# Routing written out with one-hot lists, and expert combination fused into the q/k/v projection, in a two-block transformer kernel on one Trainium2 core

## The chip, the cores and the metric

The kernel is one program on 1 core of one Trainium2 chip. The metric is the device time of one execution in microseconds (us), the median of several executions.

## The reference

1024 tokens of width 1024, all in float32. A first block mixes the tokens (latent attention and an RWKV branch), adds the product with `w_out`, normalises, and sends each token through 2 of 32 experts; a second block has windowed attention, a recurrent layer and 16 experts that choose their tokens. The part that the change touches is this:

```python
x = x + mixed @ w_out                       # x1
h2 = rms_norm(x, norm_ffn_g)
# hier_moe: best of 4 groups, best 2 of its 8 experts
group_p = softmax(h2 @ rg_w + rg_b); e_logits = h2 @ re_w + re_b
weight = gp[:, None] * tp / sum(tp); expert = gi * 8 + ti
# tokens sorted by expert, each expert's list padded to blocks of 128
slot_tok = full(cap, T).at[dest].set(stok)
y_block = (silu(xb @ w1[e]) * (xb @ w3[e])) @ w2[e]
x = x + segment_sum(yb * slot_w, slot_tok)
x = rms_norm(x, norm_final_g)               # x2, end of the first block
qkv = x @ attn_w_qkv                        # second block: rotary, window of 128, sink
x = layer_norm(ALPHA * x + attention @ attn_w_o) ...
```

## The kernel before, in words

`P = 128` tokens are a tile, `NT = 8` tiles, `KD = 8` slices of 128 of the width, `HALF = 512` columns. The program is a row of stages. Each is a `Phase`: it allocates tiles and semaphores, runs one block in which every engine (TensorE, VectorE = DVE, ScalarE = ACT, GpSimd = POOL, SyncE = SP) has its own instruction list, and ends by clearing its semaphores and a barrier of all engines (line 83 shows in the trace for it). `hold` waits on a semaphore; `link` waits for the instruction just issued, so linked vector operations run one by one. `sp.dma_start` puts a transfer on SP's queue, `act.dma_start` on ACT's, `pool.indirect_dma_start` on the software queue.

`route_phase` (L1478). SP issues eight small loads (L1544), then the first two tiles of the mixed activations (L1552), the two halves of `w_out` (L1554), the rest of the activations (L1555), and in a hardware loop x in and x1, h2 out (L1556). POOL copies each tile of activations to `m_t` (L1577). TensorE makes 16 products (128x128 by 128x512) into the one tile `po` (L1604), then turns the h2 of the tile before (8 transposes, L1612) and makes 8 logits products (L1619). The vector engine adds x (L1658), takes the norm with two short ACT steps (L1660 to L1665), scales the turned h2 (L1670) and keeps the logits (L1675). `po`, `x1`, `h2` and `h2T` exist once. When all logits are there, the vector engine makes the choice for the eight tiles at once (L1697 to L1721), three products give each token's rank in its expert (L1632 to L1634), and from it come slot numbers (`slot_u`, L1742), the expert of each block (`block_e`, L1748) and the pairs of blocks in use (`pair_used`, L1751). POOL writes the token numbers to these slots in DRAM with 16 indirect stores (L1589).

`experts_phase` (L1758). For each of up to 48 blocks, two per step: SP loads a column of 128 token numbers (L1810) and, four blocks ahead, the expert's three matrices, 3 MB (L1816, L1818); POOL gathers the 128 rows of h2 (L1823), two blocks ahead; TensorE turns them (L1845), makes 8 gate/up products (L1861), turns the hidden values and makes 4 down products (L1885). Here 32 blocks are in use.

`combine_phase` (L1982). For each tile POOL gathers two rows of results per token (L2024); the vector engine adds them with their weights to x1 (L2047, L2048), ACT takes squares and root, the vector engine normalises (L2066), SP stores x2.

`gqa_project` (L2110). In a loop over tiles: x2 in (L2143), transposes (L2171), a copy (L2235), 24 products in three groups of 512 columns (L2190), between the first and second group the transposes of the heads of the tile before (L2178, L2182); ACT copies q (L2221), the vector engine k and v (L2247, L2248) and rotates q and k (L2257 to L2263). `gqa_attend` (L2271) loads one mask per tile (L2298), its vector work begins at L2392. After it a phase of its own loads the output weights (L3004, called from L2106), and the tail's first products (L2547) wait for them.

## Time and profile before

| | us |
|---|---|
| median of 3 runs | 4951.96 (4951.84 to 4953.2) |
| profiled execution, its own time | 4939.51 |
| its span | 4937.7 |
| TensorE matmul busy | 4243.3 (86%) |
| VectorE busy | 1567.0 (32%) |
| ScalarE busy | 1090.8 (22%) |
| GpSimd busy | 290.2 (6%) |

The profile is of one execution; its time is compared with the runs' median separately. TensorE is busy for 86% of the span, so a stage in which it is idle or at the lower granted clock stands out. Rows of stages give, for each engine, busy time and instruction records (x), then TensorE's granted clock as a share of full speed, the share of the 16 DMA engines, and GB/s. Rows of the timeline give start, duration, engine, line, operation, tiles, and in brackets the idle time before and what ended it.

### The profile page before, as it was taken

To read this page: it belongs to the slowest core of one execution; us is meant where nothing else is said; L and a number is where in the kernel's file an instruction comes from. 1 tells how busy PE (TensorE), PEld (TensorE's weight loads), DVE (VectorE), ACT (ScalarE), POOL (GpSimd) and SP (SyncE) were. 2 spreads that over 40 slices of the span, in tenths; PEclk is the share of its full clock that TensorE was granted. 3 is DMA by queue.
4 is the path that set the end of the run, shared out by engine and by line. 5 is a ranking of instruction groups with operands and counts; after the bars stand their busy time and mean duration, and the time that the engine had idled before them with its cause. 6 is when DMAs were issued, how large, how long until landed. Compare 5 with 4: busy or idle time off the path is not lost. (4 is left out here: it accounts for less than half of the span.)

```text
span 4937.7 us, 63014 instructions
## 1 busy us (share of the span) xinstructions
PE 4243.3 (86%) x23058; PEld 2190.4 (44%) x23059; DVE 1567.0 (32%) x2896; ACT 1090.8 (22%) x1837; POOL 290.2 (6%) x297
## 2 busy tenths in 40 slices
PE   7899996888987849984988969999969995999996
PEld 4555445774433424442444534444434443444442
DVE  3355463542221122223165530110136536100112
ACT  1155223442100101111044300000026522000002
POOL 0000002320000010001000000000000000000000
PEclk9899998999998869997999979999989997999998
DMA  2130145432213139975001458888731133888884
GB/s 90 54 143 24 49 162 135 89 68 77 93 35 115 64 128 370 357 265 208 17 14 72 173 185 311 304 309 313 247 112 43 64 112 131 304 313 309 311 305 174
DMA packets 427020, 820.70 MB, mean 166 GB/s; under 512 B 146640, under 2 KB 288080, under 8 KB 393808
## 3 DMA queue, kind: packets, MB, share of 16 engines
q1 hardware_dynamic: 397968, 717.33, 41.9%
q0 software_dynamic: 17216, 60.83, 4.3%
q10 hardware_dynamic: 11648, 39.88, 2.0%
q8 instruction: 137, 2.24, 0.2%
q14 instruction: 51, 0.42, 0.0%
HBM read 692.09 MB, written 125.86 MB: 166 GB/s over the span
## 5 line engine op out<-in xcount | busy, mean ns | idle before, releaser
L2829 PE MATMUL ec1e_pg<-ec_wg,ec1e_xT 128*128 128x512 f32 x1024 | 445.2, 595 | 2.2 <-DVE ec1e_xT L2882 2.2
L2829 PE MATMUL ec0e_pg<-ec_wg,ec0e_xT 128*128 128x512 f32 x1024 | 444.5, 595 | 2.1 <-DVE ec0e_xT L2882 2.1
L2829 PEld LDWEIGHTS ec1e_pg<-ec_wg,ec1e_xT 128*128 128x128 f32 x1024 | 195.6, 191 | 249.0 <-issue 249.0
L2829 PEld LDWEIGHTS ec0e_pg<-ec_wg,ec0e_xT 128*128 128x128 f32 x1024 | 195.4, 191 | 248.3 <-issue 248.3
L1371 PE MATMUL mix_pb<-h_h_all,mix_wg 128*128 128x512 f32 x512 | 223.3, 597 | 12.2 <-DMA mix_wg<-in_w_in_dram 12.2
L1861 PE MATMUL exp_pg<-exp_wb,exp_xT 128*128 128x512 f32 x512 | 224.9, 598 | 6.4 <-DMA exp_wb<-in_w_dram 6.4
L3113 PE MATMUL lrui_pA<-lrui_xT,lrui_w 128*128 128x512 f32 x512 | 223.1, 595 | 2.6 <-ACT lrui_xT L3187 2.6
L2855 PE MATMUL ec1e_py<-lru_wd,ec1e_hidT 128*128 128x512 f32 x512 | 223.4, 594 | 0.0
L2855 PE MATMUL ec0e_py<-gqaw_wd,ec0e_hidT 128*128 128x512 f32 x512 | 223.4, 594 | 0.0
L679 PE MATMUL front_pz<-h_h_all,front_w 128*128 128x512 f32 x480 | 211.6, 599 | 8.8 <-DMA front_ones<-in_head_ones_dram 8.8
L2190 PE MATMUL gqap_pq<-gqap_w,gqap_xT 128*128 128x512 f32 x384 | 180.7, 631 | 22.4 <-DVE gqap_xT L2235 17.5
L1604 PE MATMUL route_po<-route_wo,route_m_t 128*128 128x512 f32 x256 | 130.8, 676 | 40.9 <-DMA route_wo<-in_w_out_dram 25.3
L2870 ACT ACTIVATE ec1e_sg<-ec1e_pg 128x512 f32<-128x512 f32 x32 | 19.1, 598 | 650.9 <-PE ec1e_pg L2829 650.9
L2870 ACT ACTIVATE ec0e_sg<-ec0e_pg 128x512 f32<-128x512 f32 x32 | 19.1, 598 | 649.8 <-PE ec0e_pg L2829 649.8
L1371 PEld LDWEIGHTS mix_pb<-h_h_all,mix_wg 128*128 128x128 f32 x512 | 98.0, 192 | 135.6 <-issue 135.6
L2890 DVE TENSOR_TENSOR ec0e_hid<-ec0e_sg,ec0e_pg 128x512 f32<-128x512 f32 x32 | 22.0, 689 | 428.1 <-ACT ec0e_sg L2870 428.1
L2890 DVE TENSOR_TENSOR ec1e_hid<-ec1e_sg,ec1e_pg 128x512 f32<-128x512 f32 x32 | 22.0, 688 | 427.3 <-ACT ec1e_sg L2870 427.3
L1861 PEld LDWEIGHTS exp_pg<-exp_wb,exp_xT 128*128 128x128 f32 x512 | 98.1, 192 | 130.2 <-issue 130.2
L3113 PEld LDWEIGHTS lrui_pA<-lrui_xT,lrui_w 128*128 128x128 f32 x512 | 97.6, 191 | 125.1 <-issue 125.1
L972 POOL TENSOR_TENSOR wkv_a_l<-wkv_a_raw,wkv_tab 128x512 f32<-128x512 f32 x80 | 106.4, 1363 | 783.5 <-ACT wkv_a_raw L988 783.5
L679 PEld LDWEIGHTS front_pz<-h_h_all,front_w 128*128 128x128 f32 x480 | 91.3, 192 | 127.1 <-issue 127.1
L2855 PEld LDWEIGHTS ec1e_py<-lru_wd,ec1e_hidT 128*128 128x128 f32 x512 | 96.0, 190 | 115.5 <-issue 114.8
(533 smaller groups left out, 6135.5 us busy)
## 6 DMA issues: line engine op xcount, KB each, us to landing
ec_wg<-in_moe_w_gate_up_dram SPq DMA_DIRECT2D x256, 1024.0 KB, 6.4
exp_wb<-in_w_dram SPq DMA_DIRECT2D x64, 1024.0 KB, 15.2
gqaw_wd<-in_moe_w_down_dram SPq DMA_DIRECT2D x128, 512.0 KB, 4.4
lru_wd<-in_moe_w_down_dram SPq DMA_DIRECT2D x128, 512.0 KB, 4.4
exp_w2b<-in_w_dram SPq DMA_DIRECT2D x32, 1024.0 KB, 14.2
wkv_inp<-arrays SPq DMA_DIRECT2D x160, 128.0 KB, 3.0
arrays<-front_out SPq DMA_DIRECT2D x36, 512.0 KB, 5.7
yb<-mlaa_zero SPq DMA_DIRECT2D x1, 16384.0 KB, 52.8
```

The lines of the kernel that those rows point to most:

```text
L679: m = nc.tensor.matmul(pz[q % 2][:, half * HALF:(half + 1) * HALF], w[:, q % U, k, :], hT[:, k, half * HALF:(half + 1) * HALF], start=k == ...
L972: nc.gpsimd.tensor_tensor(grid(a_l[:, n, :]), grid(a_raw[:, :]), mask(n + 1), ALU.mult).then_inc(a_masked, 1)
L1371: m = nc.tensor.matmul(ps[:, half * HALF:(half + 1) * HALF], weights[:, k, :], rhs[:, k, half * HALF:(half + 1) * HALF], start=k == 0, sto ...
L1604: m = nc.tensor.matmul(po[:, half * HALF:(half + 1) * HALF], m_t[:, k, :], wo[:, k, half * HALF:(half + 1) * HALF], start=k == 0, stop=k = ...
L1861: m = nc.tensor.matmul(pg[:, u, :], xT[:, b, k, :], wb[:, b, :, k, :], start=k == 0, stop=k == KD - 1)
L2190: m = nc.tensor.matmul(pq[:, b, :], xT[:, k, :], w[:, k, b * HALF:(b + 1) * HALF], start=k == 0, stop=k == KD - 1)
L2829: return nc.tensor.matmul(pg[:, b, :], xT[:, k, :], wg[:, k, b * HALF:(b + 1) * HALF], start=k == 0, stop=k == KD - 1)
L2855: m = nc.tensor.matmul(py[:, b * HALF:(b + 1) * HALF], hidT[:, k, :], wd[:, k, b * HALF:(b + 1) * HALF], start=k == 0, stop=k == KD - 1)
L2870: nc.scalar.activation(sg[:, half * HALF:(half + 1) * HALF], pg[:, half, :], ACT.Silu).then_inc(silu, 1)
L2890: nc.vector.tensor_tensor(hid[:, cols], sg[:, cols], pg[:, 2 + half, :], ALU.mult).then_inc(hid_ready, 1)
L3113: m = nc.tensor.matmul(pA[:, bank, :], w[:, q % W_RING, k, :], xT[:, k, halves[h]], start=k == 0, stop=k == KD - 1)
```

## The change: what it does

- Loads of the router: activations first, then each weight half followed by an x tile, then seven small loads. All but the last-named are no longer waited for by the first product.
- The router's loop is written out, without POOL's copy; `po`, `x1`, `h2`, `h2T` double; transposes and logits of a tile stand between the halves of the next one's product; additions go by halves.
- The choice is made for tiles 0 to 5 inside the loop, and for 6 and 7 behind it.
- The experts of the first two blocks are worked out first, and SP loads their weights then. Token lists come from 16 products of one-hot matrices, end in SBUF (`moe.idx`), and POOL gathers the first two blocks' rows in the same phase. In the experts POOL copies an index column before each gather.
- The combination phase goes; its steps stand in the projection, written out by tiles. x2 is turned from SBUF, and stored to DRAM beside that. The gathered rows lie in `oT`, the q weights in the tile `wd`.
- Three kinds of mask in place of eight; output weights are loaded at the start of attention.

```diff
 route_phase, sync:
+                sp.dma_start(mT[:, :, 0:EARLY], mix_view[:, :, 0:EARLY]).then_inc(early, 16)
+                for h in range(2):
+                    sp.dma_start(wo[:, :, halves[h]], w_out[0, :, halves[h]].rearrange("(k p) n -> p k n", p=P)).then_inc(wo_in[h], 16)
+                    sp.dma_start(xt[:, h, :], x[h * P:(h + 1) * P, :]).then_inc(x_in[h], 16)
...
+                sp.wait_ge(first_e, 1)
+                for s in range(2):
+                    e = moe.expert_of(sp, s)
+                    moe.load_gu(sp, s, e)
+                    moe.load_dn(sp, s, e)
 route_phase, gpsimd:
-                    nc.gpsimd.tensor_copy(m_t[:, :, :], mT[:, :, ds(i * P, P)]).then_inc(m_in, 1)
...
-                for n in range(2 * NT):
-                    pool.indirect_dma_start(slot_tok, bass.IndirectOffsetOnAxis(ap=slot_u[:, n:n + 1], axis=0),
-                                            tok[:, n % NT:n % NT + 1], None).then_inc(scattered, 16)
+                pool.wait_ge(idx_ready, 1)
+                for s in range(2):
+                    pool.indirect_dma_start(moe.xg[:, s, :], None, h2_dram, bass.IndirectOffsetOnAxis(ap=moe.idx[:, s:s + 1], axis=0)).then_inc(moe.x_in[s], 16)
 route_phase, tensor:
+                for t in range(NT):
+                    product(t, 0, range(KD))
+                    if t:
+                        turn_h2(t - 1)
+                    product(t, 1, range(KD // 2))
+                    if t:
+                        logits(t - 1)
+                    product(t, 1, range(KD // 2, KD))
...
+                for j in range(2 * NT):
+                    if j % NT == 0:
+                        pe.wait_ge(pos_ready, j // NT + 1)
+                    m = nc.tensor.matmul(pt[:, 0:MOE_BLOCKS], at_pos[:, j, :], in_block[:, j, :], start=j == 0, stop=j == 2 * NT - 1)
 route_phase, vector:
+                for t in range(NT):
+                    norm(t)
+                    if t + 1 < NT:
+                        add(t + 1, 0)
+                    scaled(t)
+                    keep_logits(t)
+                    if t == NT - 3:
+                        choose(0, NT - 2)
+                    if t + 1 < NT:
+                        add(t + 1, 1)
+                choose(NT - 2, NT)
...
+                experts_of(0, 2)
+                dve.sem_inc(first_e, 1)
...
+                V.link(nc.vector.tensor_tensor(in_block[:, :, :], slot_f[:, :].unsqueeze(2).to_broadcast(wide), blocks.unsqueeze(1).to_broadcast(wide), ALU.is_ge))
+                V.link(nc.vector.tensor_reduce(base[:, :], in_block[:, :, :], AX_X, ALU.add))
+                V.link(nc.vector.tensor_scalar(base[:, :], base[:, :], float(P), float(P), ALU.mult, ALU.subtract))
+                V.link(nc.vector.tensor_tensor(pos[:, :], slot_f[:, :], base[:, :], ALU.subtract))
+                V.link(nc.vector.tensor_tensor(in_block[:, :, :], base[:, :].unsqueeze(2).to_broadcast(wide), blocks.unsqueeze(1).to_broadcast(wide), ALU.is_equal))
+                for m in range(2):
+                    mine = slice(m * NT, (m + 1) * NT)
+                    nc.vector.tensor_tensor(in_block[:, mine, :], in_block[:, mine, :],
+                                            tab[:, TAB + P:TAB + P + NT].unsqueeze(2).to_broadcast([P, NT, MOE_BLOCKS]), ALU.mult)
+                dve.sem_inc(in_ready, 1)
+                for m in range(2):
+                    V.link(nc.vector.tensor_tensor(at_pos[:, mine, :], pos[:, mine].unsqueeze(2).to_broadcast([P, NT, P]),
+                                                   tab[:, TAB:TAB + P].unsqueeze(1).to_broadcast([P, NT, P]), ALU.is_equal))
+                    dve.sem_inc(pos_ready, 1)
+                experts_of(2, MOE_BLOCKS)
...
+                dve.wait_ge(i_psum, 1)
+                V.link(nc.vector.tensor_copy(moe.idx[:, 0:MOE_BLOCKS], pt[:, 0:MOE_BLOCKS]))
 experts_phase, sync:
+                def load(i, q, ahead):
+                    for u in range(2):
+                        b = 2 * q + u
+                        e = moe.expert_of(sp, i * R + (b + ahead))
+                        S.hold(gu_psum, done(i, b + ahead - R))
+                        moe.load_gu(sp, b, e)
+                        S.hold(y_psum, done(i, b + ahead - R))
+                        moe.load_dn(sp, b, e)
                 with sp.Fori(0, NB // R) as i:
+                    with sp.If(in_use(sp, i * 2 + 1) > 0):
+                        load(i, 1, 0)
+                    with sp.If(in_use(sp, i * 2 + 2) > 0):
+                        load(i, 0, R)
 experts_phase, gpsimd:
+                                nc.gpsimd.tensor_copy(ic[s][:, :], moe.idx[:, ds(i * R + (b + 2), 1)]).then_inc(ic_ready, 1)
 gqa_project, tensor:
+            for i in range(NT):
+                product(i, 0)
+                if i:
+                    turn_heads(i - 1)
+                product(i, 1)
+                if i + 1 < NT:
+                    turn_x(i + 1)
+                product(i, 2)
 gqa_project, vector:
+            for i in range(NT):
+                if i + 1 < NT:
+                    combined(i + 1)
+                if i:
+                    keep_k(i - 1)
+                if i + 1 < NT:
+                    keep_x(i + 1)
+                copy_kv(i)
+                rotate(i)
 gqa_attend:
-    mask = ph.sb("mask", [P, NT, BAND])
+    mask = ph.sb("mask", [P, 3, BAND])
...
+            load_w_out(sp, wd, w_out, wo_in)
```

`combined(i)` has the operations of L2047, L2048, L2053, L2063 and L2066, in place on x1, and waits for ACT's square and root in it. ACT runs, per tile, the square and root of tile i+1, the copy of the first half of q, the copy of the turned heads of tile i-1, and the second half of q. SP stores x2 of tile i, waits for its transposes, and loads x1 of tile i+4.

## Rows read from the trace of the kernel before

**Rows 1.** Busy time by stage: two router tiles, experts, combination, two projection tiles.
```profile
core 0: us, PE busy (x) PEld busy (x) DVE busy (x) ACT busy (x) POOL busy (x), PEclk, DMA share, GB/s
1589.50:1609.20 19.70, 16.79 (x56) 8.79 (x56) 2.49 (x5) 3.92 (x5) 1.04 (x1) 1.00 0.24 81
1609.20:1633.10 23.90, 19.73 (x56) 9.88 (x56) 3.72 (x6) 3.92 (x5) 1.04 (x1) 0.86 0.18 66
1853.00:1877.00 24.00, 23.79 (x71) 11.56 (x70) 5.81 (x9) 3.23 (x5) 1.90 (x2) 1.00 1.07 375
2220.30:2272.30 52.00, 0.00 (x0) 0.00 (x0) 31.73 (x40) 13.38 (x26) 19.18 (x17) 0.50 0.86 333
2307.00:2332.40 25.40, 23.32 (x73) 11.53 (x72) 5.12 (x19) 2.04 (x3) 0.00 (x0) 1.00 0.06 21
2332.40:2359.70 27.30, 24.67 (x71) 11.77 (x69) 5.12 (x19) 2.01 (x2) 0.00 (x0) 0.94 0.06 19
```

**Rows 2.** Who waited for whom in the router: us in total, times, longest.
```profile
PE route_po L1604 <- DVE route_x L1658: 15.6, 7, 2.4
```

**Rows 3.** Timeline, start of the router, SP's queue and TensorE.
```profile
1555.98 0.35 SPq L1549 DMA_DIRECT2D route_ident<-in_eye_dram  x1
...
1560.44 0.43 SPq L1552 DMA_DIRECT2D route_mT<-mixT  x1
...
1572.58 15.45 PE L1604 MATMUL route_po<-route_wo,route_m_t 128*128 128x512 f32 x32 [25.35 <-DMA route_wo<-in_w_out_dram]
```

**Rows 4.** Timeline, last tile of the router.
```profile
1752.64 1.23 DVE L1658 TENSOR_TENSOR route_x<-route_po,route_xt 128x1024 f32<-128x1024 f32 x1 [0.52 <-issue]
...
1759.00 0.75 DVE L1665 TENSOR_SCALAR route_h<-route_x,route_small 128x1024 f32<-128x1024 f32 x1 [0.37 <-DVE route_small L1662]
...
1763.10 3.62 PE L1619 MATMUL route_pl<-route_rw,route_h2T 128*128 128x36 f32 x16 [1.32 <-DVE route_h2T L1670]
1766.76 0.20 DVE L1675 TENSOR_TENSOR route_lg<-route_pl,route_rb 128x36 f32<-128x36 f32 x1 [3.72 <-PE route_pl L1619]
```

**Rows 5.** Timeline, rank products and slots.
```profile
1777.73 1.22 PE L1632 MATMUL route_pr<-route_mem,route_tab 128*128 128x256 f32 x2 [11.01 <-DVEq L1721]
...
1780.19 0.42 DVE L1731 TENSOR_TENSOR route_over<-route_pl,route_tab 128x256 f32<-128x256 f32 x1 [1.38 <-PE route_pl L1634]
...
1784.41 1.76 DVE L1745 TENSOR_TENSOR route_cmp<-route_pend,route_tab 128x1536 f32<-128x1536 f32 x1 [0.15 <-DVE slots L1742]
```

**Rows 6.** Timeline, token lists to the first expert product.
```profile
1784.61 2.60 POOL L1589 DMA_INDIRECT slot_tok<-route_tok,slots  x1 [60.22 <-DVEq L1743]
...
1813.14 0.98 POOL L1823 DMA_INDIRECT exp_xg<-h,exp_idx  x1 [6.79 <-DMA exp_idx<-slot_tok]
...
1818.23 1.94 PE L1845 MATMUL exp_pt<-exp_ident,exp_xg 128*128 128x128 f32 x8 [38.15 <-DMA exp_xg<-h,exp_idx]
...
1829.95 5.30 PE L1861 MATMUL exp_pg<-exp_wb,exp_xT 128*128 128x512 f32 x6 [6.36 <-DMA exp_wb<-in_w_dram]
```

**Rows 7.** Combination and projection: timeline, and one row of DMA issues (us to landing last).
```profile
2220.32 0.35 SPq L2003 DMA_DIRECT2D comb_g<-in_norm_final_g_dram  x1
...
2232.10 1.28 DVE L2047 SCALAR_TENSOR_TENSOR comb_x<-comb_ya,weights,comb_x 128x1024 f32<-128x1024 f32 x1 [22.75 <-DMA comb_ya<-yb,slots]
...
2238.71 1.28 DVE L2066 SCALAR_TENSOR_TENSOR comb_out<-comb_x,comb_small,comb_g 128x1024 f32<-128x1024 f32 x1
...
2283.58 16.63 PE L2190 MATMUL gqap_pq<-gqap_w,gqap_xT 128*128 128x512 f32 x32 [4.92 <-DMA gqap_w<-in_attn_w_qkv_dram]
...
2495.99 0.76 DVE L2247 COPY gqap_ks<-gqap_pq 128x256 f32<-128x256 f32 x2 [13.04 <-PE gqap_pq L2190]
...
comb_ya<-yb,slots POOLq DMA_INDIRECT x16, 10.0
```

**Rows 8.** Timeline, start of attention and of the tail.
```profile
2509.35 0.17 DVE L2392 TENSOR_SCALAR gqaa_nsk<-gqaa_sk 128x16 f32<-128x16 f32 x1 [7.22 <-DMA gqaa_sk<-in_attn_sink_dram]
...
2684.17 2.24 SPq L3004 DMA_DIRECT2D gqaw_wd<-in_attn_w_o_dram  x4
...
2692.19 22.31 PE L2547 MATMUL ec0p_po<-gqaw_wd,gqa_oT 128*128 128x512 f32 x48 [9.67 <-DMA gqaw_wd<-in_attn_w_o_dram]
```

More of the change, by code:

```diff
@@ L1465 @@
 LOGITS = N_GROUPS + N_EXP
+D_EXP = 256
 def route_tables():
@@ L1618, in logits @@
                     for k in range(KD):
[L1619 removed]
+                        m = nc.tensor.matmul(pl[:, 0:LOGITS], h2T[:, t % 2, k, :], rw[:, k, :], start=k == 0, stop=k == KD - 1)
                     m.then_inc(l_psum, 1)
[L1623 to L1627 removed]
+                pe.wait_ge(early, 16)
```

734 lines of the change are left out of this document (341 added, 393 removed).

## The prediction

> **What bounds the kernel now.** I read the table of stages first, then the waits, then the timeline at the seams. The stages touched lie in a row from 1556 to 2692 us, one after another behind barriers, so whatever a stage loses ends on the total.
>
> In the output product and router, the reader is to see two tiles [rows 1]: one at a granted clock of 1.00 has 16.8 us of TensorE work; the next ones last 23.9 us with 19.7 us of work at a mean of 0.86. So 4.2 us per tile are idle, and 2.9 us are the same work at the lower of the two levels (1.2 GHz). The engine waits up to 2.4 us for the vector engine's addition out of the only PSUM tile [rows 2]. All experts are at 99% TensorE and near the DMA limit as well (375 GB/s). The combination does no TensorE work at all for 52 us, and the q/k/v projection repeats the router's pattern: 27.3 us per tile, 23.3 us of work at clock 1.00, 24.7 at 0.94 [rows 1].
>
> **Part 1, order of loads.** Eight small transfers stand ahead of the big ones, from 1555.98 to 1560.44, and the product starts at 1572.58, when the first half of the weights is there [rows 3]. Now the activations go first, and the product waits for weights alone. A 0.5 MB x tile stands only in front of the second half, whose need is 8.6 us later (the 15.5 of the first product less the 6.9 of a half at full clock). Gain 4.5 us. Bounds: nothing (if bandwidth, not issue, sets it) and 4.5.
>
> **Part 2, the tiles of the router.** From the first product to the last addition it takes 180.1 us [rows 3, 4]. PSUM, x, h2 and h2T are now double, the POOL copy is gone, and transposes and logits of tile t-1 stand inside the product of tile t. Does the vector engine keep up? Addition to finished h2 takes 7.1 us (1752.64 to 1759.75) [rows 4]; the addition by halves takes 0.6 us off, so 6.5 us, against 6.9 us for the next half product (a tile's 16.8 less 1.0 for transposes and 1.8 for logits, half of the 1.94 and 3.62 at the lower clock [rows 4, 6]; half of the 13.9 left). The scaling (1.2 us) lies behind the next 3.4 us. So no wait, and no fall of the clock: first product 15.5, then 7 x 16.8 = 117.6 us. Where it goes wrong is the choice for tiles 0 to 5, put between the logits of tile 5 and the second addition of tile 6. All eight tiles took from 1766.96 to 1777.73 for 41 operations, 0.26 us each [rows 4, 5]; 29 operations make some 7.7 us, only 3.4 of which are covered, so h2 of tile 6 comes 14.2 us after those logits (0.4 + 7.7 + 0.7 for the half addition + 5.4 to h2) and TensorE is free for it at 10.3 (3.4 + 6.9): 3.9 us idle, after which I expect the clock down, 3 us (the 2.9 of rows 1). Sum 140.0, gain 40.1 us, and 0.6 for the last half addition. Bounds: 47 us if that stall were nothing, 30 if each tile kept 1.5 us.
>
> **Part 3, the choice at the end** is for two tiles: 25 operations of 0.2 us (0.20 is the 36-element addition [rows 4]), 5.3 us for 10.8. Gain 5.4.
>
> **Part 4, lists.** Before: from the first operation behind the rank products (1780.19) the slots are ready at 1784.4, then POOL writes 16 index columns, SP fetches them back, the gather starts at 1813.14, its rows are turned at 1818.23, and the first expert product waits for weights until 1829.95: 49.8 us [rows 5, 6]. After, counted from the same operation: blocks of the experts 1.6; the first two expert numbers 2.4 (weights of two blocks, 6 MB, leave here and need 16 us at 375 GB/s, so they are no longer last). Slots at 4.4. Vector operations go by 0.15 us plus 1.05 ns per element (256 elements 0.42, 1536 elements 1.76 [rows 5]): three of 768 elements 3.0, two small 0.4, two of 384 1.1, the first of 1024 1.25; so 10.2 us. Then 16 products of 48 columns: the nearest row is 8 products of 36 columns at the lower clock, 3.6 us [rows 4], so 7.8 us, 18.0. (The second 1024 and 46 expert numbers, 1.2 + 3.9 us, lie beside them.) Copy and semaphore 18.5; gather to first turn 5.1 as before, 23.9; the barrier lies beside it. Turn, scale, second turn: 29.5 us, where rows alone had 11.7 from turn to product because of the weights. Gain 20.3. Bounds 12 to 26: gather as slow as 10.0 us [rows 7], or products at full clock.
> The Trainium skill, DMA: Bandwidth & Descriptors, section on the anatomy of one software DMA, fits 2.0 us plus bytes over 436 GB/s; that is 3.2 us for a 512 KB gather where the row has 5.1, and by it the gain would be 1.9 us more.
>
> In the experts themselves nothing on TensorE changes; POOL copies the index column (under 0.5 us) and gathers two blocks, some 23 us, ahead, and SP loses two small fetches. Cost 0; if that cover went, each block would pay the gather's 5 to 10 us. The new outer phase adds one barrier; at most the 1.65 us between TensorE's last work (2692.19 - 9.67 = 2682.52) and SP's first issue at 2684.17 [rows 8]; I take 1.0 loss.
>
> **Part 5, combination inside the projection.** Before, stage start 2220.32, first combination 2232.10, first projection product 2283.58: 63.3 us [rows 7]. After: rows land as before 11.8 (more is queued on SP's queue behind the first x tile, not ahead of it; SP's queue was full then too); combination to normalised 7.9 (2232.10 to 2239.99); turn 1.9, copy 1.2, wake-ups 0.6: 23.4. Gain 39.9. Weights: w0, w1, w2 are needed at 23, 32 and 40 us; all 13 MB of gathers, x1 and weights take 35 us at 375 GB/s plus 2 of latency; at the 333 GB/s of the old combination [rows 1] 41: between 0 and 3 us of stall, taken as 0 since the last of it is an x1 tile. On SP a store of x2 now waits for the turn, and the x1 load behind it, three tiles ahead: hidden by 23 us per tile. ident, g and the table go to ACT's queue, needed at 18 us.
> Per tile, the vector engine has 7.4 us of combination with its waits for ACT, 1.9 of copies, 1.2 of k/v, 3 of rotation: 13.5 of 23.3, and the combination of i+2 is done 12 us after the last product of i, where TensorE asks for it at 15.4. So 23.3 per tile: from first product to end of the last, 212.4 us before [rows 7], now 8 x 23.3 = 186.4. Gain 26.0. Bounds 0 and 28.
>
> **Part 6, attention.** Masks shrink from 1.5 to 0.56 MB; the first vector operation waited 7.2 us for them and the sinks [rows 8]. The 4 MB of output weights come behind. Gain 2.3, bounds 0 and 4. The tail's first product waited 9.7 us for these weights, from which 1.7 us to SP's first issue stay [rows 8]: gain 7.9; next late is the x tile, needed only 8.6 us after, a half product at the lower clock.
>
> **Sum.** -4.5 -40.1 -0.6 -5.4 -20.3 +1.0 -39.9 -26.0 -2.3 -7.9 = -146.0 us. The profiled execution took 4939.5 (span 4937.7), so it would be 4793.5; the median of the runs, 4951.96, lies 12.5 above it, and from it the forecast is 4806.
>
> **Rivals.**
> A, the projection waits for the vector engine or ACT each tile (x late, or ACT's root standing ahead of the q copy): it keeps 27.3 per tile, 4806 + 26 = 4832. Against: 13.5 of 23.3 us. Chance 0.08.
> B, routing and lists dearer: router tiles each keep a 1.5 us wait and lists cost 8 us more: 4806 + 10 + 8 = 4824. For: margin of 0.4 us in part 2. Chance 0.12.
> C, better than forecast: no clock loss at the early choice, gather and products quick, no low clock at the tail's start (about 2): 4806 - 7 - 6 - 2 = 4791. Chance 0.12.
> D, slower than before: SP's queue in the experts. Loads for the next pair now stand in the present iteration behind holds on its own blocks' products. Were they no longer ahead, each of 15 pairs would show its 6 MB, 16 us at 375 GB/s: +240, less 146, 5046 us. It decides from 146 / 15 = 9.7 us exposed per pair. For: the stage moves 375 GB/s with the DMA share at 1.07 [rows 1], so lateness isn't made up. Against: the counts held are those of four blocks earlier, as before. Chance 0.03.
> E, the change doesn't do what it says: the weights fetched in attention or the expert prefetch are waited for all the same. Then 4806 + 8 + 6 = 4820. Chance 0.03.
> Forecast 0.62.
>
> **How the numbers follow.** Range 4780 to 4838: C and B inside, A's value inside, ends by the bounds of parts 2 and 4. Out: D and mishaps together. A measurement here tells 0.2% (10 us) from no change. Only D ends above: faster 0.95, same 0.01, slower 0.04.
>
> **What would show it.** Right: router tiles 16.8 us apart at clock 1.00 and one gap of 4 us at tile 6; 18 us from rank to index list; first expert product about 29.5 us after; experts at 99% TensorE from the first product on; no stage without TensorE between experts and projection beyond 24 us; tiles there 23.3 us; no wait for output weights. Wrong: waits of TensorE in the experts for weights, granted clock under 0.95 in router or projection, or the first row gather landing later than 15 us.

## The result: 158.8 us less, and the profile after

The kernel after takes 4793.08 us (median of 4 runs, 4791.92 to 4793.86), the kernel before in the same series 4951.9 (4949.94 to 4953.2): ratio 0.968, 95% interval 0.966 to 0.970, or 158.8 us less where 146.0 were forecast. It is well inside the range of 4780 to 4838. A second series gave 0.968 again (0.967 to 0.969).

The profiled execution after took 4792.43 us (span 4790.5, mean granted clock 0.945 for 0.933). Its difference to the profiled execution of before is only 147.1 us, because the profiled execution of before was a quick one, in two places that the change doesn't touch. The mixing stage issued its last store at 1551.78 us there and at 1558.39 here, and what lies behind the tail's first product took 2245.5 us there and 2249.6 here. Both numbers move from one execution to the next whatever the kernel: in the 13 profiles of this study they lie between 1551.8 and 1560.8, and between 2245.5 and 2251.2. Between these two points, from 1551.78 to 2692.19 before and from 1558.39 to 2540.91 after, lie 1140.4 and 982.5 us: 157.9 less, which is what the medians say. All that follows is told by that stretch, which I call the touched stretch:

| from ... to | before | after | measured | forecast |
|---|---|---|---|---|
| mixing's last store, router's first product | 20.8 | 15.8 | -5.0 | -4.5 |
| to the start of the last addition | 180.1 | 131.0 | -49.1 | -40.1 |
| to the last logits kept | 14.1 | 9.4 | -4.7 | -0.6 |
| choice, rank products, to the first list operation | 13.4 | 8.05 | -5.4 | -5.4 |
| to the first expert product | 49.8 | 32.9 | -16.9 | -20.3 |
| experts and their end | 390.4 | 389.7 | -0.7 | +1.0 |
| to the first projection product | 63.3 | 21.9 | -41.4 | -39.9 |
| projection, to the copy behind the last product | 212.4 | 185.6 | -26.8 | -26.0 |
| turn of the last heads, phase change | 7.0 | 8.0 | +1.0 | 0 |
| attention | 180.0 | 178.9 | -1.2 | -2.3 |
| to the tail's first product | 9.2 | 1.25 | -8.0 | -7.9 |

Two rows flatter the change a little, for this execution was quick there. In a second profile of the same kernel (`after_again`) the row "to the start of the last addition" has 132.0 us and "to the last logits kept" 10.3; the second number comes back in the six variants below that leave this part of the router as it is.

Busy times by stage, of the kernel after: two router tiles, experts, two projection tiles (columns as in [rows 1]).

```profile
core 0: us, PE busy (x) PEld busy (x) DVE busy (x) ACT busy (x) POOL busy (x), PEclk, DMA share, GB/s
1602.30:1618.70 16.40, 16.40 (x59) 8.70 (x58) 3.87 (x7) 1.35 (x3) 0.00 (x0) 1.00 0.28 96
1775.00:1799.00 24.00, 23.75 (x71) 11.48 (x70) 5.29 (x8) 3.22 (x5) 2.31 (x4) 1.00 1.06 380
2194.20:2216.90 22.70, 22.70 (x69) 11.18 (x68) 9.16 (x24) 3.44 (x6) 1.89 (x2) 1.00 0.36 116
2216.90:2239.70 22.80, 22.80 (x70) 11.22 (x69) 9.20 (x24) 3.44 (x6) 1.90 (x2) 1.00 0.28 92
```

Against [rows 1] TensorE has no idle time left in a tile, 16.4 of 16.4 us and 22.8 of 22.8, at the higher level of the clock (granted clock 1.00). The experts are as they were.

Timeline of the router after: the start, the tile behind the early choice, the last tile.

```profile
1562.42 0.40 SPq L1579 DMA_DIRECT2D route_mT<-mixT  x1
...
1574.16 22.26 PE L1624 MATMUL route_po<-route_wo,route_mT 128*128 128x512 f32 x48 [20.32 <-DMA route_wo<-in_w_out_dram]
...
1695.37 1.09 PE L1635 MATMUL route_pt<-moe_ident,route_h 128*128 128x128 f32 x8 [0.57 <-DVE route_h L1707]
...
1705.15 0.69 DVE L1696 TENSOR_TENSOR route_x<-route_po,route_xt 128x512 f32<-128x512 f32 x1 [3.32 <-PE route_po L1624]
...
1707.25 0.20 ACT L1680 ACTIVATE route_small<-route_small 128x1 f32<-128x1 f32 x1 [0.22 <-DVE route_small L1701]
...
1707.68 0.75 DVE L1707 TENSOR_SCALAR route_h<-route_x,route_small 128x1024 f32<-128x1024 f32 x1
...
1714.57 0.20 DVE L1720 TENSOR_TENSOR route_lg<-route_pl,route_rb 128x36 f32<-128x36 f32 x1 [3.72 <-PE route_pl L1643]
```

The reader is to see the 0.57 us in front of the transposes of tile 6 (1695.37). That is nearly the whole price of the early choice (0.8 us by the kernel without it, below), where 3.9 us and a fall of the clock were forecast; the first products behind it run at 0.45 us each, and the granted clock there is 1.00, the higher level (2.4 GHz). And from addition to finished h2 the last tile takes 3.3 us (1705.15 to 1708.43) where [rows 4] have 7.1. In the last tile the transposes (1708.49) took 1.09 us behind a wait of 3.38 us, so at the higher level. In the second profile of the same kernel the same wait was followed by the lower one:

```profile
1709.90 1.97 PE L1635 MATMUL route_pt<-moe_ident,route_h 128*128 128x128 f32 x8 [3.38 <-DVE route_h L1707]
```

These 0.9 us are the whole difference between 9.4 and 10.3 us in that tile.

Timeline of the lists after.

```profile
1722.62 0.42 DVE L1775 TENSOR_TENSOR route_over<-route_pl,route_tab 128x256 f32<-128x256 f32 x1 [2.65 <-PE route_pr L1664]
...
1732.91 7.03 PE L1670 MATMUL route_pt<-route_in_block,route_at_pos 128*128 128x48 f32 x32 [10.33 <-DVEq L1812]
...
1741.22 1.13 POOL L1612 DMA_INDIRECT moe_xg<-h,moe_idx  x1 [612.09 <-DVEq L1818]
...
1742.65 0.96 POOL L1612 DMA_INDIRECT moe_xg<-h,moe_idx  x1 [0.30 <-issue]
...
1750.24 1.94 PE L1900 MATMUL exp_pt<-moe_ident,moe_xg 128*128 128x128 f32 x8 [10.29 <-PEq L83]
...
1755.53 2.04 PE L1916 MATMUL exp_pg<-moe_wb,exp_xT 128*128 128x512 f32 x2
```

The list is complete and the first gather leaves 18.6 us behind the first list operation, as forecast (18.5). But the first turn of rows waits for line 83, the change of phase, not for the rows: it comes 27.6 us behind the first list operation (1750.24), where 23.9 were forecast.

Timeline of the projection, the attention's start and the tail's start after.

```profile
2145.25 0.35 SPq L2107 DMA_DIRECT2D gqap_x<-x  x1
...
2160.74 1.28 ACT L2202 ACT_TABLE_LOAD   x1
...
2167.16 9.00 PE L2164 MATMUL gqap_pq<-gqa_wd,gqap_xT 128*128 128x512 f32 x16 [1.32 <-DVE gqap_xT L2243]
2179.24 7.13 PE L2164 MATMUL gqap_pq<-gqa_wd,gqap_xT 128*128 128x512 f32 x16 [3.08 <-DMA gqa_wd<-in_attn_w_qkv_dram]
...
2352.80 0.76 DVE L2254 COPY gqap_ks<-gqap_pq 128x256 f32<-128x256 f32 x2 [13.04 <-PE gqap_pq L2164]
...
2366.81 0.18 DVE L2410 TENSOR_SCALAR gqaa_nsk<-gqaa_sk 128x16 f32<-128x16 f32 x1 [6.94 <-DMA gqaa_sk<-in_attn_sink_dram]
...
2540.91 20.84 PE L2566 MATMUL ec0p_po<-gqa_wd,gqa_oT 128*128 128x512 f32 x48 [1.70 <-PEq L83]
```

Three things are to be seen: a wait of 3.08 us for the weights of the second group of products (taken as 0, bounded by 3); the sinks (8 KB, one number per head for the softmax), still waited for almost as long as before (6.94 for 7.22 in [rows 8]) though the masks have shrunk to 0.56 MB; and the tail's first product, which waits for nothing but the phase change.

### The profile page after: what moved, and what is told of

It is laid out like the page before. It is cut to its first block and busy times, and to the rows that moved or that the text cites. A ratio compares the mean times of both kernels' runs of the same rounds, so it can differ in the third digit from the quotient of the medians.

```text
span 4790.5 us, 62335 instructions
## 1 busy us (share of the span) xinstructions
PE 4221.4 (88%) x23090; PEld 2185.5 (46%) x23091; DVE 1579.2 (33%) x2933; ACT 1072.3 (22%) x1830; POOL 267.3 (6%) x304
## 5 line engine op out<-in xcount | busy, mean ns | idle before, releaser
L2874 PE MATMUL ec0e_py<-gqa_wd,ec0e_hidT 128*128 128x512 f32 x512 | 223.3, 594 | 0.0
L2874 PEld LDWEIGHTS ec0e_py<-gqa_wd,ec0e_hidT 128*128 128x128 f32 x512 | 96.0, 190 | 115.3 <-issue 114.8
L1371 PE MATMUL mix_pb<-mix_oT,mix_wb 128*128 128x512 f32 x256 | 119.1, 629 | 32.9 <-DMA mix_wb<-in_w_br_rwkv_dram 30.9
L459 PE MATMUL mlaa_pS<-mla_kT,mla_qT 96*128 96x512 f32 x256 | 129.7, 631 | 4.6 <-ACT mlaa_probs L522 2.5
L1624 PE MATMUL route_po<-route_wo,route_mT 128*128 128x512 f32 x256 | 114.4, 601 | 20.3 <-DMA route_wo<-in_w_out_dram 20.3
```

The source lines that it names most:

```text
L459: m = nc.tensor.matmul(pS[:, u % 2 * 2 + j, :], q_all[:, head, tile * P:(tile + 1) * P], k_all[:, head, j * HALF:(j + 1) * HALF], start=Tr ...
L1371: m = nc.tensor.matmul(ps[:, half * HALF:(half + 1) * HALF], weights[:, k, :], rhs[:, k, half * HALF:(half + 1) * HALF], start=k == 0, sto ...
L1624: m = nc.tensor.matmul(po[:, t % 2, halves[h]], mT[:, k, t * P:(t + 1) * P], wo[:, k, halves[h]], start=k == 0, stop=k == KD - 1)
L2874: m = nc.tensor.matmul(py[:, b * HALF:(b + 1) * HALF], hidT[:, k, :], wd[:, k, b * HALF:(b + 1) * HALF], start=k == 0, stop=k == KD - 1)
```

## The experiments

A kernel's own runs spread by 2 to 14 us here, so that medians tell 10 us and not 3. Where a few microseconds matter I read the stage. The touched stretch is 982.5 us in the profile after, and 985.0 in a second one, so it repeats to some 3 us; "longer" below is against the 982.5. None of these kernels leaves out a part of the computation. In each text, "4801.74 us for 4950.19" gives the median of the variant and that of the kernel before in the same series, and the ratio's 95% interval stands behind it.

### The baseline again

> The kernel after, unchanged, as the baseline of this group of kernels. The mixing stage ahead of the change ended at 1551.8 to 1558.4 us in the profiled executions so far, whichever kernel it was, so single executions differ by some 7 us; median expected 158 us under the kernel before.

4791.24 us (4789.04 to 4801.97, 5 runs), ratio 0.9679 (0.9665 to 0.9692); in its series the kernel before took 4954.65. The mixing stage's last store lay at 1551.8 to 1560.8 in the profiles of this study, with and without the change (1556.7 in the next kernel, which is the one before but for a loop; 1552.0 and 1552.4 in two with the change). So the 6.6 us there between the two first profiles are a difference of executions.

### ScalarE's table loads, taken out of the kernel before

```diff
-                with act.Fori(0, NT) as i:
+                for i in range(NT):
```

> The kernel before, with only ScalarE's loop of the router written out (eight times square and root), nothing else. Theory, a hardware loop reloads ScalarE's function table in each turn because its body is entered with an unknown table, and written-out code doesn't: the loads at the two router lines fall from 16 to one or two, the norm from addition to h2 takes about 4.5 us for 7.1, the tiles keep their distance of 23.9 us (the norm lies beside the product), and only the last tile gains: from the last addition to the kept logits 11.7 us for 14.3, the whole kernel -3 us (4949). Rival, the loads went away because of something else in the change (double tiles, or the order of the other engines): 16 loads, 14.3 us, total unchanged. In either case the mixing stage ahead ends where it does in the profile of before (1551.8) if the 6.6 us by which it ended later after the change come from the changed program, and can lie some us off if they are spread between executions.

4947.71 us for 4950.19, ratio 0.9997 (0.9988 to 1.0007). ScalarE's groups in the router, of the kernel before and then of this one (line, engine, operation, count, busy us, mean ns, idle before):

```profile
L1641 ACT ACT_TABLE_LOAD x8 | 10.3, 1283 | 324.7 <-DVE route_x L1658 324.7
L1643 ACT ACT_TABLE_LOAD x8 | 10.3, 1283 | 3.2 <-DVE route_small L1660 3.2
```

```profile
L1643 ACT ACTIVATE route_small<-route_small 128x1 f32<-128x1 f32 x8 | 1.6, 203 | 2.4 <-DVE route_small L1660 2.3
...
L1643 ACT ACT_TABLE_LOAD x1 | 1.3, 1283 | 0.0
```

Its last tile, from the addition to the kept logits:

```profile
1759.15 1.22 DVE L1658 TENSOR_TENSOR route_x<-route_po,route_xt 128x1024 f32<-128x1024 f32 x1 [0.52 <-issue]
...
1761.89 0.20 ACT L1643 ACTIVATE route_small<-route_small 128x1 f32<-128x1 f32 x1 [0.33 <-DVE route_small L1660]
...
1770.54 0.20 DVE L1675 TENSOR_TENSOR route_lg<-route_pl,route_rb 128x36 f32<-128x36 f32 x1 [3.72 <-PE route_pl L1619]
```

Sixteen loads of 1.28 us have become one, and that tile takes 11.4 us for 14.1 [rows 4]: 2.7 less, the two loads in it. The form of the loop alone does it. In the total the 3 us that were expected can't be told from nothing: the ratio's interval holds 1, and the touched stretch is 1141.8 us for 1140.4, within what single executions differ by. The Trainium skill, page "ScalarE activation tables: per-element evaluation and per-set limits", section on table sets in the compiler and the runtime, says that the back end places table loads block by block; this pair of profiles agrees, if a loop's body is such a block (it pays its loads in each turn, the written-out list once).

### The table loads, put back into the kernel after

```diff
                     act.wait_ge(ms, t + 1)
+                    nc.scalar.activation(spare[:, :], small[:, u, 1:2], ACT.Exp, scale=1e-6)
                     nc.scalar.activation(small[:, u, 2:3], small[:, u, 1:2], ACT.Sqrt).then_inc(root, 1)
```

> The kernel after, with an extra exponential of one column between square and root of each router tile, so that two table loads and an instruction (2.8 us) stand in each norm again. Theory, the stall at the early choice was small (0.57 us where 3.9 and a fall of the clock were forecast) because the norm had lost its table loads: the wait of TensorE for h2 of tile 6 grows to 3 us or a little more, the clock may fall behind it (another 3), the last tile takes 2.8 us more (9.6 to 12.4 from addition to kept logits), the other tiles stay 16.4 us apart: total +5.5 us without a fall of the clock, +8.5 with one. Rival, the stall was small because the choice itself is covered otherwise: the wait stays below 1 us and the total goes up by 2.8 only. Second rival, the norm is short of the half product in every tile: tiles over 17 us apart, total +15 or more.

4801.74 us for 4950.19, ratio 0.9692 (0.9675 to 0.9709). The median is 8.7 us above that of the kernel after (theory 8.5 with a fall of the clock), and the touched stretch is 994.1 us, 11.6 longer. Behind the early choice:

```profile
1697.38 1.97 PE L1636 MATMUL route_pt<-moe_ident,route_h 128*128 128x128 f32 x8 [3.17 <-DVE route_h L1709]
1699.14 5.75 PE L1625 MATMUL route_po<-route_wo,route_mT 128*128 128x512 f32 x8
```

The wait is 3.17 us for 0.57, and behind it the transposes take 1.97 us for 1.09 and eight records of products 5.75 for 3.60: the clock has fallen to the lower level (1.2 GHz) and comes back within them. That is 3.2 us of wait and 3.0 of clock, where the forecast had 3.9 and 3.0. All earlier tiles kept 16.4 us, and from first product to last addition it is 137.3 us (1572.85 to 1710.15) for 131.0; the 0.7 not named yet lie in the first tile (23.0 for 22.3), which takes 22.3 to 23.9 us in the profiles with the change. The last tile takes 12.9 us for 9.4 (1710.15 to 1723.03): 2.6 are the loads, and 0.9 the transposes at the lower clock, which `after_again` has too. The theory holds, with the clock's fall: 5.6 us at tile 6 and 2.6 in the last one. The remaining 3.4 us of the stretch's 11.6, with the 0.7 and the 0.9 in them, are differences of executions as far as the profiles show.

### Without the early choice

```diff
-                    if t == NT - 3:
-                        choose(0, NT - 2)
...
-                choose(NT - 2, NT)
+                choose(0, NT)
```

> The kernel after, with the choice made for all eight tiles behind the loop and none inside. By the trace after, the choice for six tiles takes 7.3 us in 29 operations, so for eight 31 operations take some 8.0 us in place of the 5.3 for two, and the stall of 0.57 us in the loop goes: total +2 us. The larger part of what the forecast put down to doing six tiles early (10.8 to 5.3 us) then comes from the choice's own fewer operations (31 for 41). Rival, the prediction's account, the early choice costs a stall and low-clock time of several us: without it the kernel gains 4 us. Second rival, the early choice is worth all 5.5 us: total +5.

4796.22 us for 4950.19, ratio 0.969 (0.9674 to 0.9706); touched stretch 986.6, 4.1 longer. From the last logits kept to the rank products it takes 8.7 us (1709.58 to 1718.29) for 5.5 (1714.57 to 1720.08), and the loop, without the choice in it, is 0.8 us quicker (first transposes to last addition 108.1, 1591.19 to 1699.30, for 108.9). So the early choice is worth 2.4 us net, as the theory has it (2), and of the 5.4 that part 3 had for it 2.2 come from the choice's fewer operations. The stretch shows 4.1, of which 0.9 are the last tile's transposes at the lower clock (1.97 us for 1.09), which `after_again` has as well; the rest is within its 3 us.

### The first gathers behind the phase change

```diff
 route_phase, gpsimd:
-                pool.wait_ge(idx_ready, 1)
-                for s in range(2):
-                    pool.indirect_dma_start(moe.xg[:, s, :], None, h2_dram, bass.IndirectOffsetOnAxis(ap=moe.idx[:, s:s + 1], axis=0)).then_inc(moe.x_in[s], 16)
 experts_phase, gpsimd, ahead of the loop:
+                for s in range(2):
+                    pool.indirect_dma_start(xg[:, s, :], None, h2_dram, bass.IndirectOffsetOnAxis(ap=moe.idx[:, s:s + 1], axis=0)).then_inc(x_in[s], 16)
```

> The kernel after, with the first two gathers of rows issued at the start of the experts' phase, behind the phase change, instead of ahead of it. After the change the engines stood still from POOL's last issue at 1743.6 to 1750.2 us. Theory, the phase change waits for the gathers in flight on POOL's queue: without them it takes 1.7 us, the gathers leave 3 us later than now and land in the same 6 us, so that the first turn of rows stands within 1 us of where it is (27.6 us behind the first list operation), total 0 to +1. Rival, the phase change waits for SP's weight transfers (6 MB, in flight until 1748) or takes 6.6 us for other reasons: the gathers leave at 1750 and the first turn comes at 1756, total +6.

4795.81 us for 4950.19, ratio 0.9687 (0.9671 to 0.9704); touched stretch 985.9. The seam between the phases (the list was copied at 1741.87):

```profile
1743.30 0.17 DVE L1823 TENSOR_TENSOR weights<-weights,route_e 128x8 f32<-128x8 f32 x1
1745.31 1.13 POOL L1882 DMA_INDIRECT moe_xg<-h,moe_idx  x1 [615.16 <-POOLq L83]
...
1750.39 1.97 PE L1899 MATMUL exp_pt<-moe_ident,moe_xg 128*128 128x128 f32 x8 [8.63 <-DMA moe_xg<-h,moe_idx]
...
1754.82 1.97 PE L1899 MATMUL exp_pt<-moe_ident,moe_xg 128*128 128x128 f32 x8 [2.46 <-DMA moe_xg<-h,moe_idx]
1756.78 5.53 PE L1915 MATMUL exp_pg<-moe_wb,exp_xT 128*128 128x512 f32 x8
```

With no gather in flight the phase changes in 1.8 us (1743.47 to 1745.31), and this while the DMA engines still carried the 6 MB of weights (398 GB/s from 1743.5 to 1745.3, DMA share 1.07). From the copied list to the first turn it takes 8.5 us for 10.2, to the first product 14.9 for 15.5. So issuing the gathers ahead of the phase change, as the change does, gains nothing at this seam; the theory had the turn within 1 us of where it was, and it came 1.7 us sooner.

### The first experts' weights loaded in their own phase

```diff
 route_phase, sync:
-                for s in range(2):
-                    e = moe.expert_of(sp, s)
-                    moe.load_gu(sp, s, e)
-                    moe.load_dn(sp, s, e)
 experts_phase, sync, ahead of the loop: the same four lines
```

> The kernel after, with the weights of the first two blocks loaded at the start of the experts' phase (SP, 1751) instead of at 1726 in the routing. Theory, these 6 MB are then the last thing that the first product waits for, as before the change, where from SP's first weight issue (1815.1) to that product (1829.95) it took 14.8 us: first product at about 1766 for 1755.5, +10, and since the stage took 379.4 us from there before the change and 378.2 after, nothing is lost or made up later: total +10. Rival, the transfers are a second bound of the experts (375 GB/s, share 1.07) and the 16 us that 6 MB need are never made up: +16. Second rival, only the 2 MB of the first block's gate and up weights count and the rest hides: +4.

4799.21 us (4793.46 to 4801.21), ratio 0.9697 (0.9682 to 0.9712); touched stretch 996.7, 14.2 longer.

```profile
1738.55 0.96 POOL L1608 DMA_INDIRECT moe_xg<-h,moe_idx  x1 [0.30 <-issue]
1745.08 1.94 PE L1900 MATMUL exp_pt<-moe_ident,moe_xg 128*128 128x128 f32 x8 [9.23 <-PEq L83]
1745.20 1.03 SPq L1502 DMA_DIRECT2D moe_wb<-in_w_dram  x2
...
1759.22 9.76 PE L1916 MATMUL exp_pg<-moe_wb,exp_xT 128*128 128x512 f32 x16 [8.85 <-DMA moe_wb<-in_w_dram]
```

14.0 us from SP's first issue to the product (14.8 expected), and 10.0 us more than after from the router's first product to this one (191.4 for 181.4). That is the theory's number; from there to the projection's first product it takes 413.5 us for 411.6, so the 6 MB are neither made up nor paid twice. (Another 2 us lie in projection and attention, which this edit doesn't touch.) The same rows settle the experiment before: no weights are in flight here, only the two gathers, and the engines still stand from 1739.5 to 1745.1; the DMA engines carry nothing from 1743.0 on, and 2 us later the next phase begins. Both ways round, it is POOL's gathers in flight that hold the change of phase. What in the change of phase waits for them isn't shown.

### The turn of the next tile behind the products

```diff
-                if i + 1 < NT:
-                    turn_x(i + 1)
                 product(i, 2)
+                if i + 1 < NT:
+                    turn_x(i + 1)
```

> The kernel after, with the transposes of the next tile moved in the projection from ahead of the third group of products to behind it, as before the change. Theory, the tile distance fell from 27.3 to 22.8 us because no copy of turned rows stands between two products any more: now the copy (1.2 us) and its two wake-ups (0.4) are open again in 7 tiles, 1.6 us each, distance 24.4 us, total +11; with a fall of the clock behind each wait up to +20. Rival, the distance fell because q, k and v are copied by groups out of a PSUM tile that is asked for in turn, and the place of the transposes is hidden: +2 or less.

4798.16 us (4792.72 to 4800.74) for 4947.61, ratio 0.9695 (0.9681 to 0.971); touched stretch 993.3, 10.8 longer.

```profile
2194.19 7.13 PE L2164 MATMUL gqap_pq<-gqa_wd,gqap_xT 128*128 128x512 f32 x16 [1.32 <-DVE gqap_xT L2243]
...
2218.56 7.13 PE L2164 MATMUL gqap_pq<-gqa_wd,gqap_xT 128*128 128x512 f32 x16 [1.32 <-DVE gqap_xT L2243]
```

24.37 us from tile to tile for 22.79, and 196.6 us from the first product to the last copy for 185.6: the theory's 24.4 and +11, with no fall of the clock at waits of 1.3 us. Of the 4.6 us that a tile lost (27.35 to 22.79), 1.6 are the hidden copy of the turned rows. The other 3.0 stand in the trace of the kernel before:

```profile
2332.45 0.76 DVE L2247 COPY gqap_ks<-gqap_pq 128x256 f32<-128x256 f32 x2 [13.04 <-PE gqap_pq L2190]
...
2334.06 1.23 DVE L2235 COPY gqap_xT<-gqap_pt 128x1024 f32<-128x1024 f32 x1 [0.53 <-DVE gqak_v L2248]
...
2335.68 8.80 PE L2190 MATMUL gqap_pq<-gqap_w,gqap_xT 128*128 128x512 f32 x16 [2.63 <-DVE gqap_xT L2235]
```

There the copies of k and v stand ahead of the copy of the turned rows, so TensorE waits 2.6 us and not 1.3; and behind that wait 16 records take 8.8 us and not 7.1, for the clock is at the lower level at first (granted clock 0.62 in the first 4.3 us). In this experiment the change's order of copies stays, so both stay away: 1.3 and 1.7 us. That the order does it is read from these rows; no kernel has it alone.

### The second half of the change alone

Routing and experts of the kernel before, with the projection, masks and attention of the kernel after.

> The kernel before, with the second half of the change alone: combination in the projection, three masks, output weights in the attention; routing and experts as before. By the traces, from the start of the stage behind the experts to the tail's first product it took 471.9 us before (2220.3 to 2692.2) and 395.7 after (2145.25 to 2540.9): total -76 against before, and the other half of the change then is worth 83. Rival, the halves work on each other (the first gather or the weights land otherwise behind the old experts' phase): the stage differs from 395.7 by over 3 us.

4871.06 us (4867.45 to 4880.15) for 4947.61, ratio 0.9851 (0.9836 to 0.9866): 76.6 us less. From SP's first load to the tail's first product 396.7 us (2221.64 to 2618.3), for 395.7 in the whole change, so the theory holds (the rival asked for over 3 us of difference). The rest of the 158.8, some 82 us, is the routing half: the touched stretch of the two first profiles has 81.7 of them ahead of the projection's stage (668.5 us before, 586.9 after). No kernel with the routing half alone was run, and its largest item, the router's tiles (23.9 to 16.4 us), wasn't taken apart into doubled tiles, copies by halves and the new order: that these remove the waits of [rows 2] is read from the traces.

### The output weights behind the attention

```diff
 gqa_attend, sync:
-            load_w_out(sp, wd, w_out, wo_in)
 gqa_phase, ahead of layer_tail:
+        load_w_out(nc.sync, wd, w_out, wo_in)
```

> The kernel after, with the output weights loaded behind the attention again. Theory, the forecast's term of 7.9 us: from the attention's last vector operation to the tail's first product 9.2 us for 1.25, and the engine's clock is lower at the start of the tail (its first 48 products 22.3 us for 20.8): +8 at the seam, +9.5 in all. Rival, the 4 MB also take bandwidth from the start of the attention (masks and sinks landed only 6 us in), and that is given back: +7.

4805.67 us (4799.44 to 4807.82), ratio 0.9701 (0.9688 to 0.9715), against 0.9679 (0.9665 to 0.9692) in the same series; touched stretch 990.5, 8.0 longer.

```profile
2368.80 0.17 DVE L2410 TENSOR_SCALAR gqaa_nsk<-gqaa_sk 128x16 f32<-128x16 f32 x1 [4.69 <-DMA gqaa_sk<-in_attn_sink_dram]
```

```profile
2551.30 23.92 PE L2566 MATMUL ec0p_po<-gqa_wd,gqa_oT 128*128 128x512 f32 x48 [9.34 <-DMA gqa_wd<-in_attn_w_o_dram]
```

From the attention's last vector operation (2542.41) to this product it takes 8.9 us for 1.25, and its 48 records take 23.9 us for 20.8. But the sinks come 3.7 us behind the attention's start (2365.1), not 6.0, and the attention is 1.6 us shorter (177.3 for 178.9): the rival is right as well. Together that makes 7.6 - 1.6 + 3.1 = 9.1 us, between the theory's 9.5 and the rival's 7; the medians lie 14.4 apart, more than these seams account for. The 4 MB stand behind masks and sinks on SP's queue, and the sinks are slowed all the same: from issue to landing they take 5.6 us with the 4 MB behind them and 3.4 without, the masks 3.5 and 3.3. Before the change the sinks came after 6.4 us; three masks alone would have saved 2.7 of these, and the weights behind them give 2.3 back.

### What is left at these seams, first try

```diff
+            mask = kept.sb("mask", [P, 3, BAND])
+            sk = kept.sb("sk", [P, NQ])
 gqa_project, sync, behind the first loads:
+            sp.dma_start(mask[:, :, :], masks).then_inc(early, 16)
+            sp.dma_start(sk[:, :], sink[0].partition_broadcast(P)).then_inc(early, 16)
 gqa_project, gpsimd:
-                if i >= B:
-                    pool.wait_ge(summed, i - B + 1)
+                if i >= 2:
+                    pool.wait_ge(summed, max(i - B, 0) + 1)
 gqa_project, scalar, first:
+            nc.scalar.activation(warm[:, :], wts[:, 0:1], ACT.Sqrt)
...
 gqa_attend, sync:
-            sp.dma_start(mask[:, :, :], masks).then_inc(consts, 16)
-            sp.dma_start(sk[:, :], sink[0].partition_broadcast(P)).then_inc(consts, 16)
```

> The kernel after with three small edits in the second block's first stages. One, masks and sinks are loaded behind the last load of the projection, not at the start of the attention, whose first vector operation waited 6 us for the sinks (8 KB, landed 5.6 us after issue) and then stands 1.5 us behind the start, when the first scores are there: -4.5. Two, POOL gathers the rows of tiles 2 and 3 only when tile 0 is summed, so that 2 MB less stand in the way of the weights for the second group of products, which waited 3.1 us: -3. Three, a square root of one column at the start of ScalarE's list, so that the table load of 1.28 us between the first square and root lies in idle time: -1.3. Sum -9, 4784. Rivals: the mask size or the sinks do not matter because TensorE's first scores at the lower clock set the start (-1 instead of -4.5); the wait for weights is set by the 4 MB of weights themselves and stays (0 instead of -3).

4789.47 us (4778.71 to 4789.81) for 4947.61, ratio 0.9672 (0.9659 to 0.9686); touched stretch 980.0, 2.5 shorter (5.0 than in `after_again`), where 9 were expected. First product 20.7 us behind the stage's start for 21.9, the 1.2 of the table load. The attention's first masked operation comes 3.1 us behind its start for 6.2, the first scores at the lower clock now being last. The wait for weights has only moved, from the second group to the third:

```profile
2186.71 7.13 PE L2171 MATMUL gqap_pq<-gqap_wkv,gqap_xT 128*128 128x512 f32 x16 [2.39 <-DMA gqap_wkv<-in_attn_w_qkv_dram]
```

### Second try

The other edits are those of the first try; only the hold of the gathers is another.

```diff
-                if i >= 2:
-                    pool.wait_ge(summed, max(i - B, 0) + 1)
+                if i >= 2:
+                    pool.wait_ge(p_psum, 3 * (i - 2) + 2)
+                if i >= B:
+                    pool.wait_ge(summed, i - B + 1)
```

> As a_more, with POOL's gathers for tiles 2 and later held until TensorE has finished the second group of products two tiles earlier. In a_more the hold went with the sum of tile 0, eight gathers were issued between 2160 and 2171, and the wait of 3.1 us for the second group's weights had only moved to the third group (2.4). Theory, without these gathers in the first 35 us the transfers ahead of the last weights are 10.6 MB, 26 us at the 415 GB/s seen there, and they land by 2175 where they are needed at 2186: both waits go. Against the kernel after: first product 1.2 sooner, waits -3.1, attention's start -2.8 as in a_more: -7. Rival, the gathers come late now for tiles 2 and 3 and TensorE waits for turned rows: +3 or more in the second and third tile.

```profile
2167.49 16.32 PE L2173 MATMUL gqap_pq<-gqa_wd,gqap_xT 128*128 128x512 f32 x32 [1.32 <-DVE gqap_xT L2253]
2183.65 1.04 PE L2159 MATMUL gqap_pt<-gqa_ident,gqap_x 128*128 128x128 f32 x8
2184.53 7.03 PE L2173 MATMUL gqap_pq<-gqap_wkv,gqap_xT 128*128 128x512 f32 x16
```

Both waits are gone and no later tile waits. The touched stretch is 976.3 us: 6.2 and 8.7 under the two profiles of the kernel after, where the theory had 7. In part that is luck: the attention's first scores ran at the higher clock here (8 records in 1.56 us) and at the lower one in the first try (2.93 us), 1.4 us that no edit is shown to bring. In the medians it doesn't show: 4792.56 (4787.14 to 4796.26) beside 4791.24 (4789.04 to 4801.97) in the same series, intervals of the ratio 0.9662 to 0.9688 and 0.9665 to 0.9692. So the two waits are shown to be the gathers' doing; that the whole kernel is faster is not shown.

## Why the prediction was right, and where it was off

The direction and the sum hold, and nine of the table's eleven rows are within 4 us; it fell 12.8 us short of the gain. What came is nearly rival C (4791), by two of its three mechanisms: no loss of clock at the early choice, and none at the tail's start (48 records in 20.8 us for the 22.3 of [rows 8]). Its third, a quick gather, didn't come. The reason for the first, the table loads, stood in no rival.

**Part 1** right: -5.0 for -4.5. From the last store to the first product it is 15.8 to 16.6 us in the ten profiles with this order of loads and 20.4 to 21.2 in the three without.

**Part 2** held too little, -53.8 with the last tile for -40.7 (and -51.9 by `after_again`). The step that failed is "addition to finished h2 takes 7.1 us", carried over from a loop to a written-out list. 2.6 of those 7.1 us were table loads that the change's form takes away; measured are 3.3. So the tile-6 stall was 0.57 us for 3.9 and the clock stayed up. Putting the loads back gives 6.2 us of stall and clock for the forecast's 6.9. (The forecast's own terms would give a stall of some 4.3: it takes 0.7 + 5.4 us from addition to h2 there, and 6.5 two sentences before.) The last tile loses 4.7 us in this profile: 3.8 between addition and h2, 2.6 of them the two loads, 0.5 half the addition and 0.7 not taken apart, and 0.9 by transposes at the higher clock. The last item is luck of the one execution, since seven of the eight profiles with an unchanged router don't have it. The tile itself was mis-sized by 0.4 us: 16.4, for a row of 16.8 us whose groups of products end in idle time, while in the unbroken row one group's end overlaps the start of the next by some 0.16 us. That is 3 us over seven tiles.

**Part 3** right in the sum, with half the reason: 3.2 us from doing six tiles early, of which the loop takes 0.8 back, and 2.2 from fewer operations.

**Part 4** right up to the list (18.6 us for 18.5, with 16 products at 7.0 for 7.8), wrong in "the barrier lies beside it". The phase change waits for the gathers that lie beside it, and the first turn for the phase change: -16.9 for -20.3. (18.5 and 5.1 make 23.6, not the 23.9 of the text; the 0.3 matter little.) The gathers took 5.9 us from issue to landing in the median with the weights beside them and 4.6 without, for the row's 5.1; by the Trainium skill's figure (DMA: Bandwidth & Descriptors, anatomy of one software DMA) quoted in the forecast they would have taken 3.2, and neither run agrees.

**Experts** right: nothing lost, and the prefetch is worth 10.0 us of the lists' 16.9. Rival D didn't come: TensorE in the experts waited for no weights.

**Part 5** right twice (-41.4, -26.8), the second time by two errors that cancel. The weights' wait was at its upper bound, 3.08 us, and was taken as nothing; a tile was taken as 23.3 us and takes 22.8, 3.5 us less over the seven behind the first. Eight gathers share the first 35 us with the weights, and the experiments show it is those that decide. The +1.0 behind the last product wasn't in the sum: the last transposes ran at 1.97 us, at the lower clock, and behind the same wait (3.57 us) at 1.09 before the change. Why, no run shows.

**Part 6** right for the weights (-8.0), off for the masks, -0.4 at the attention's start for -2.3. The masks' own term was well sized (2.7 without the weights); the step that failed is "the 4 MB of output weights come behind", costed at nothing, which takes 2.3 back.

## What to carry to other kernels

A duration read inside a hardware loop holds for that loop: look which of its rows (table loads, wake-ups) belong to its form before carrying it over. A change of phase waited here for software gathers in flight, so that a prefetch across it gains only what lands before; transfers on SP's queue didn't hold it. Where a stage starts with all its transfers at once, holding back what isn't needed soon removes waits (3.1 us in the stage here, nothing clear in the medians), but the hold must be tied to the consumer that is short of bandwidth, or the wait moves to the next weights. One profile is one execution: read a microsecond of clock in a second one before giving it a cause.

## What the runs showed of the hardware

- ScalarE reloaded its function table twice per turn of a hardware loop with square and root in the body (16 loads of 1.28 us in the kernel before), and once in all when the loop was written out. After a load the next activation started within 0.02 us (2237.20 behind the load of 2235.90 in the kernel before).
- POOL's gathers in flight held the change of phase for 5.6 to 6.6 us; with 6 MB in flight on SP's queue and no gather it took 1.8 us.
- The length of a wait alone doesn't tell whether TensorE's granted clock falls. It stayed at the higher level behind waits of 0.57 us, of 1.3 us once per tile, and of 2.1 us in one tile of the projection before. It was at the lower level behind 2.6 us in the projection before and 3.2 us in the router, which cost 1.7 and 3.0 us more. Behind the same 3.4 us in the router's last tile it stayed up in one profile and fell in seven.
- Large loads behind a small transfer on the same queue delayed it: the 8 KB of sinks landed 5.6 us after their issue with 4 MB behind them and 3.4 without, and were first used at 6.0 and 3.7 us.
